# VectorE's waits on itself in the branch kernels of a hybrid decoder trunk: one signal per group of independent operations

## The reference, cut to what matters

```python
u = hn @ w_in[l]
ya = _rwkv7(...) * silu(ag)      # branch A
yb = _hgrn2(...) * silu(bg)      # branch B
yc = _retention(...) * silu(cg)  # branch C
yd = _rglru(...) * silu(dg)      # branch D
merged = sum(merge_gates[:, :, b_i] * (branches[b_i] @ w_branch[l, b_i]) for b_i in range(N_BRANCH))
h = h + gate[:, None, :] * (merged @ w_out[l])
return _rmsnorm(h, final_g)
```

```python
rel = jnp.where(causal, b[:, :, :, None, :] - b[:, :, None, :, :], -jnp.inf)
scores = jnp.sum(q_c[:, :, :, None, :] * k_c[:, :, None, :, :] * jnp.exp(rel), -1)
o = einsum('bhts,bhsv->bhtv', scores, v_c) + einsum('bhtk,bhkv->bhtv', q_c * jnp.exp(b), S)
S = jnp.exp(b_end)[:, :, 0, :, None] * S + einsum('bhsk,bhsv->bhkv', k_c * jnp.exp(b_end - b), v_c)
```

## Time and profile before

| what | value |
|---|---|
| median of three runs | 1161.91 us (1161.1 to 1162.35) |
| time of the profiled execution | 1158.29 us |
| its span, first to last instruction | 1156.1 us |
| mean granted TensorE clock | 0.986 of full speed |
| busy, share of the span | TensorE 93%, weight loads 72%, VectorE 54%, ScalarE 28%, GpSimd 31% |

### The profile page before, as it was taken

The page is one execution under the profiler, slowest core; times in us unless marked ns, Lnnn a source line. Parts: engine busy times, 40 slices in busy tenths (PEclk is TensorE's granted clock), DMA queues, the critical chain, the costliest instruction groups (busy, mean ns, idle before and its releaser), DMA issues.

```text
span 1156.1 us, 23105 instructions
## 1 busy us (share of the span) xinstructions
PE 1072.9 (93%) x9924; PEld 833.6 (72%) x9924; DVE 629.2 (54%) x1033; ACT 327.6 (28%) x527; POOL 361.5 (31%) x347
## 2 busy tenths in 40 slices
PE   1799999989889999999999999999989889999997
PEld 1577786767667777777777787777777767887885
DVE  5773943785463433444443118569999676423544
ACT  4615213311322122122131034144354341001311
POOL 0442543221356222222221233342222138662000
PEclk9999999899999999999999999999999999999999
DMA  9411111110101011011110121111111017412221
GB/s 381 150 37 37 46 55 46 57 35 23 33 25 39 25 34 39 26 32 39 34 35 23 38 64 37 37 56 34 39 34 38 26 31 259 142 37 92 73 91 54
DMA packets 80101, 70.27 MB, mean 61 GB/s; under 512 B 4096, under 2 KB 72960, under 8 KB 78976
## 3 DMA queue, kind: packets, MB, share of 16 engines
q1 hardware_dynamic: 74528, 49.34, 13.7%
q10 hardware_dynamic: 5472, 19.47, 4.6%
HBM read 64.60 MB, written 4.19 MB: 60 GB/s over the span
## 4 chain that ended last, share of the span: by engine, by line
PE 72%; DVE 21%; ACT 3%; DMA 2%; issue 2%; SPq 0%; POOL 0%; DVEq 0%; ACTq 0%
PE bank L553 46%; PE bank L969 8%; PE bank L599 6%; DMA slots<-in_w_mod 1%; DVE slots L1899 1%; DVE slots L1727 1%; DVE slots L1477 1%; DVE slots L1530 1%; DVE slots L1633 1%; PE bank L788 1%; DVE stage L1873 1%; DVE stage L1631 1%; PE bank L784 1%; DMA slots<-in_x 1%; DVE stage L1867 1%
## 5 line engine op out<-in xcount | busy, mean ns | idle before, releaser
L553 PE MATMUL bank<-hn_hi,w_hi 128*128 128x512 f32 x944 | 390.8, 414 | 8.4 <-ACT slots L1038 3.1
L553 PE MATMUL bank<-hn_lo,w_hi 128*128 128x512 f32 x944 | 370.6, 393 | 0.0
L553 PE MATMUL bank<-hn_hi,w_lo 128*128 128x512 f32 x944 | 369.8, 392 | 0.0
L465 POOL CAST w_hi<-w_raw 128x512 fp32r<-128x512 f32 x118 | 82.3, 697 | 650.6 <-PE bank L553 614.8
L553 PEld LDWEIGHTS bank<-hn_hi,w_hi 128*128 128x128 f32 x944 | 178.3, 189 | 54.4 <-issue 7.6
L553 PEld LDWEIGHTS bank<-hn_hi,w_lo 128*128 128x128 f32 x944 | 178.5, 189 | 39.3
L553 PEld LDWEIGHTS bank<-hn_lo,w_hi 128*128 128x128 f32 x944 | 178.9, 189 | 33.8 <-issue 1.7
L467 POOL TENSOR_TENSOR w_lo<-w_raw,w_hi 128x512 fp32r<-128x512 f32 x118 | 161.0, 1364 | 9.4
L1060 ACT ACTIVATE stage<-bank 128x512 f32<-128x512 f32 x64 | 38.3, 598 | 219.3 <-PE bank L553 183.3
L1038 ACT ACTIVATE slots<-bank 128x512 f32<-128x512 f32 x50 | 29.9, 598 | 159.8 <-PE bank L553 159.5
L1631 DVE TENSOR_TENSOR stage<-stage,bank 128x512 f32<-128x512 f32 x48 | 33.0, 687 | 65.4 <-PE bank L599 63.8
(11 more groups left out here) (308 smaller groups left out, 1471.6 us busy)
## 6 DMA issues: line engine op xcount, KB each, us to landing
w_raw<-in_w_in SPq DMA_DIRECT2D x118, 256.0 KB, 2.9
slots<-in_w_mod SPq DMA_DIRECT2D x8, 1024.0 KB, 8.5
slots<-in_x SPq DMA_DIRECT2D x8, 512.0 KB, 7.7
w_branch<-in_w_branch SPq DMA_DIRECT2D x32, 128.0 KB, 2.9
slots<-in_w_mod ACTq DMA_DIRECT2D x8, 512.0 KB, 4.8
slots<-in_w_out ACTq DMA_DIRECT2D x8, 512.0 KB, 5.7
xr<-in_x ACTq DMA_DIRECT2D x8, 512.0 KB, 3.6
out<-xr ACTq DMA_DIRECT2D x8, 512.0 KB, 2.7
```

The lines of the kernel that those rows point to most:

```text
L465: nc.gpsimd.tensor_copy(w_hi[p][:, :, :], w_raw[p][:, :, :]).then_inc(s_w_hi_ready, 1)
L553: last = mm(o, w[p][:, k4, :], h[:, k, n * HALF:(n + 1) * HALF], start=(p == 0 and k4 == 0 and q == 0), stop=(p == 1 and k4 == 3 and q == 2))
```

## The change

VectorE no longer signals and waits after each instruction of the groups named here; within a group it waits only where an instruction reads what an earlier one wrote, and the last instruction of the group signals.

- `prep`: `b_hat` and `k_hat` are written first; `a_r` half 0, the wait for `b_hat`, `b_end`, `a_r` half 1, the wait for `k_hat`, and `k_end` follow.
- The masks `m_all` (L1675) and `Ud` (L1690): one wait, before L1694.
- `u_sb` (L1737) and G (L1749): the increments stay, since TensorE waits for them; VectorE's own waits go.
- `exponents`: one increment and one wait, at L1801. `decayed`: the same, at L1856.
- `h_prod` (L1867): one wait for both halves j. h_s (L1880): VectorE's own waits go.

Counts of TensorE's and ScalarE's waits are the same. No instruction of another engine changes, and no buffer.

```diff
-                nc.vector.tensor_tensor(ar[:, :, :, 0, :], four(4), ep[:, :, :, 0:64], MUL).then_inc(s_vector_step, 1)
-                dve.wait_ge(s_vector_step, after(s_vector_step))
-                nc.vector.tensor_tensor(ar[:, :, :, 1, :], four(8), ep[:, :, :, 1:65], MUL).then_inc(s_vector_step, 1)
-                dve.wait_ge(s_vector_step, after(s_vector_step))
                 nc.vector.tensor_tensor(jc(b_hat), four(14), jc(Em), MUL).then_inc(s_vector_step, 1)
-                dve.wait_ge(s_vector_step, after(s_vector_step))
+                b_done = after(s_vector_step)
                 nc.vector.tensor_tensor(jc(k_hat), four(10), jc(Em), MUL).then_inc(s_vector_step, 1)
-                dve.wait_ge(s_vector_step, after(s_vector_step))
+                k_done = after(s_vector_step)
+                nc.vector.tensor_tensor(ar[:, :, :, 0, :], four(4), ep[:, :, :, 0:64], MUL)
                 e_end = Ep[i % 2][:, :, 64:65].to_broadcast([P, 4, C])
-                nc.vector.tensor_tensor(b_end, b_hat, e_end, MUL).then_inc(s_vector_step, 1)
-                dve.wait_ge(s_vector_step, after(s_vector_step))
+                dve.wait_ge(s_vector_step, b_done)
+                nc.vector.tensor_tensor(b_end, b_hat, e_end, MUL)
+                nc.vector.tensor_tensor(ar[:, :, :, 1, :], four(8), ep[:, :, :, 1:65], MUL)
+                dve.wait_ge(s_vector_step, k_done)
                 nc.vector.tensor_tensor(k_end, k_hat, e_end, MUL).then_inc(s_a_ends_ready, 1)
...
-                                            MUL).then_inc(s_vector_step, 1)
-                    dve.wait_ge(s_vector_step, after(s_vector_step))
+                                            MUL)
...
                                             small_table(tb("up1"), 2), MUL).then_inc(s_vector_step, 1)
-                    dve.wait_ge(s_vector_step, after(s_vector_step))
+                after(s_vector_step)
+                dve.wait_ge(s_vector_step, after(s_vector_step))
...
                                                 ADD).then_inc(s_a_sa_ready, 1)
-                        dve.wait_ge(s_a_sa_ready, after(s_a_sa_ready))
...
                             .then_inc(s_a_g_ready, 1)
-                        dve.wait_ge(s_a_g_ready, after(s_a_g_ready))
...
-                    nc.vector.tensor_tensor(zz[:, :, :, 0:hl], mid, bb[:, :, :, 0:hl], SUB).then_inc(s_vector_step, 1)
-                    dve.wait_ge(s_vector_step, after(s_vector_step))
-                    nc.vector.tensor_tensor(zz[:, :, :, hl:2 * hl], bb[:, :, :, hl:2 * hl], mid, SUB)\
-                        .then_inc(s_vector_step, 1)
-                    dve.wait_ge(s_vector_step, after(s_vector_step))
-                nc.vector.tensor_copy(zd[:, 7, :, :], b).then_inc(s_vector_step, 1)
-                dve.wait_ge(s_vector_step, after(s_vector_step))
+                    nc.vector.tensor_tensor(zz[:, :, :, 0:hl], mid, bb[:, :, :, 0:hl], SUB)
+                    nc.vector.tensor_tensor(zz[:, :, :, hl:2 * hl], bb[:, :, :, hl:2 * hl], mid, SUB)
+                nc.vector.tensor_copy(zd[:, 7, :, :], b)
...
-                nc.vector.tensor_tensor(h_qe[i % 2], zd[:, 7, :, :], q, MUL).then_inc(s_vector_step, 1)
-                dve.wait_ge(s_vector_step, after(s_vector_step))
+                nc.vector.tensor_tensor(h_qe[i % 2], zd[:, 7, :, :], q, MUL)
                 nc.vector.tensor_tensor(zd[:, 8, :, :], zd[:, 8, :, :], k, MUL).then_inc(s_b_z_ready, 1)
...
-                        dve.wait_ge(s_vector_step, after(s_vector_step))
+                    after(s_vector_step)
+                    dve.wait_ge(s_vector_step, after(s_vector_step))
...
                                                    op1=ADD).then_inc(s_b_s_ready, 1)
-                    dve.wait_ge(s_b_s_ready, after(s_b_s_ready))
```

More of the change, by code:

```diff
@@ L1844, in decayed @@
                     qq = q.rearrange("p j (n s) -> p j n s", s=2 * hl)
-                    nc.vector.tensor_tensor(zz[:, :, :, 0:hl], zz[:, :, :, 0:hl], kk[:, :, :, 0:hl], MUL)\
-                        .then_inc(s_vector_step, 1)
-                    dve.wait_ge(s_vector_step, after(s_vector_step))
+                    nc.vector.tensor_tensor(zz[:, :, :, 0:hl], zz[:, :, :, 0:hl], kk[:, :, :, 0:hl], MUL)
                     nc.vector.tensor_tensor(zz[:, :, :, hl:2 * hl], zz[:, :, :, hl:2 * hl],
-                                            qq[:, :, :, hl:2 * hl], MUL).then_inc(s_vector_step, 1)
-                    dve.wait_ge(s_vector_step, after(s_vector_step))
-                nc.vector.tensor_copy(e_last[i % 2], zd[:, 7, :, P - 1:P].rearrange("p j t -> p (j t)"))\
-                    .then_inc(s_vector_step, 1)
-                dve.wait_ge(s_vector_step, after(s_vector_step))
-                nc.vector.tensor_tensor(h_qe[i % 2], zd[:, 7, :, :], q, MUL).then_inc(s_vector_step, 1)
-                dve.wait_ge(s_vector_step, after(s_vector_step))
+                                            qq[:, :, :, hl:2 * hl], MUL)
+                nc.vector.tensor_copy(e_last[i % 2], zd[:, 7, :, P - 1:P].rearrange("p j t -> p (j t)"))
+                nc.vector.tensor_tensor(h_qe[i % 2], zd[:, 7, :, :], q, MUL)
                 nc.vector.tensor_tensor(zd[:, 8, :, :], zd[:, 8, :, :], k, MUL).then_inc(s_b_z_ready, 1)
```

## The result

| | before | changed kernel |
|---|---|---|
| median, first comparison (4 runs each) | 1161.51 us | 1144.49 us (1143.98 to 1147.27) |
| profiled execution, its span | 1158.29, 1156.1 us | 1144.64, 1142.8 us |
| ratio to before, 95% interval | | 0.986, 0.9841 to 0.988 |
| four repeats, 24 runs, medians | 1158.37, 1160.04, 1159.08, 1159.63 us | 1148.04, 1148.27, 1148.27, 1147.56 us |
| ratios of the repeats | | 0.9908, 0.9904, 0.9914, 0.9902 (each within 0.9882 to 0.9931) |

The change is faster. The four repeats gave 10.3, 11.8, 10.8 and 12.1 us off, 11.2 in the mean. So there are two things to explain: the gain, and why one comparison was 6 us beside the repeats.

What follows compares the result with a forecast made beforehand. The prediction took TensorE as the bound, with VectorE late in branch B from pass 1 on. Its terms 9.3 + 1.45 + 0.3 = 11.05 us, off the median of 1161.91, gave 1150.9 us, range 1148.2 to 1156.0.

Steps and rivals of the forecast that it cites:

- The six waits of L929: Branch B: TensorE's waits for ScalarE's L1269, held up by late VectorE, all go: 9.3 us.
- The 1.45 us of clock: Branch B, pass 6: the clock fall behind the longest wait of L929 goes too, 1.45 us.
- The estimate of 0.10 us a wait: Price of one VectorE self-wait, taken below ScalarE's 0.14 us; 35 make 3.5 us a pass of branch B.
- point of saturation: Branch B: the first pass makes up its 1.98 us once each of 35 waits is worth 0.057 us.
- only the gap goes: Rival: one VectorE self-wait is worth 0.03 us, VectorE stays late, 1155.5 us; chance 0.14.
- nothing goes: Rival: VectorE drains between instructions with or without a wait, so the time stays 1161.9 us; chance 0.07.
- slower: Rival: VectorE groups without gaps keep GpSimd out, the weight split is late, TensorE waits: 1164.9 us; chance 0.03.
- 9.7 us of room: Branch B: time from the end of GpSimd's weight split to its first use; only a longer hold costs.
- forecast 0.3: Branch A, pass 0: three fewer self-waits on VectorE's way to L1696, 0.3 us, between 0 and 0.57.
- costed at nothing: Branch A, passes 1 to 7: 14 self-waits a pass go or move, covered by TensorE's fill, worth nothing.
- the low end of the range: 1148.2 us: adds 0.27 us in branch A, another 1.45 us of clock and 1 us of scatter.
- The sum, 11.05 us: Whole kernel: 9.3 for waits of L929, 1.45 for clock, 0.3 for branch A's pass 0; chance 0.74.

Runs made afterwards that it cites:

- masks_only: The kernel before with only the self-waits of the masks m_all and Ud in branch A removed: 1157.6 us, ratio 0.9986.
- before_again: The kernel before, run and profiled once more with nothing changed: 1158.6 us, ratio 1.0.
- b_rep: Repeat of the kernel before with only branch B's edits (exponents, decayed, h_prod, h_s): 1147.2 us, ratio 0.9902.
- exp_only: The kernel before with only the self-waits of branch B's exponents removed, 15 a pass: 1150.8 us, ratio 0.9927.
- dec_only: The kernel before with only the self-waits of branch B's decayed operands removed, 16 a pass: 1148.7 us, ratio 0.992.
- a_only: The kernel before with only branch A's edits (prep, masks, Ud, u_sb, G): 1156.5 us, ratio 0.998.
- b_only: The kernel before with only branch B's edits (exponents, decayed, h_prod, h_s): 1145.8 us, ratio 0.9883.

## Why the prediction was right or wrong

**Right: where the time goes.** The six waits of L929 are gone; pass 0 to pass 6 shortened by 9.14 us, forecast 9.3. The last pass, with the longest wait and the clock fall behind it, shortened by (144.10 - 122.97) - (133.60 - 113.83) = 1.36 us, forecast 1.45. Together 10.5 us, forecast 10.75. The passes take 18.97 us in the mean, forecast 18.9, though not all are near it (18.42 to 19.83), and the clock of the stretch is 1.00. No wait of L929 for another engine took the place. The 1.45 us of clock came out by luck, in part: the forecast read them from one execution. With the same waits of L929 or nearly, masks_only had no fall in B, and before_again had two; b_rep, without these waits, had one.

**Right: that the exact price hardly matters, but its size was low.** The estimate of 0.10 us a wait measured 0.12. exp_only (15 waits, 1.85 us by that price) and dec_only (16, 1.97 us) each bring nearly all that 35 waits bring, and keep 2.7 and 1.7 us of waits. The forecast put the point of saturation at 0.057 us for each of 35 waits, 1.98 us a pass in the first pass; both stand right at it. Nothing of the rivals "only the gap goes" and "nothing goes" is left: the starts moved by 0.12 us, not by 0.03 or 0. The rival "slower" was wrong in its size and not in its mechanism. GpSimd's records in B are longer (44 of 50.43 us in all, where 43 of 35.28 us stood), and the traces show where: a cast of L465 that starts within the group L1838 and L1839 takes 2.17 us, where the casts of the kernel before took 0.61 to 0.76.

```profile
796.19 2.17 POOL L465 CAST w_hi<-w_raw 128x512 fp32r<-128x512 f32 x1 [7.78 <-PE bank L553]
```

In all five profiles of the changed kernel five or six of B's casts take 2.1 to 2.2 us. So a group without waits does keep GpSimd back, by 1.6 us here, against the 9.7 us of room that the prediction read; no L553 or L599 waits for it there.

"VectorE: DVE Perf Modes" of the Trainium skill, section "The DRAIN you can't avoid", would by its eight copies have made the gain zero; for tensor_tensor of 128 columns this trace differs, and the measurement decides. The same section also says that a next operation that is not held starts earlier, which the prediction left out; the 375 overlapping records agree with that. The estimate from the Trainium skill's "Vector Engine (DVE) Microarchitecture Reference", section "Measured stream behaviour on trn2", 208 ns from start to start, agrees with the 203 measured.

**Right, but seen in the traces alone: branch A.** In pass 0 from the first L1674 to L1695 VectorE now takes 1.91 us, and it took 2.30: 0.39 us sooner, forecast 0.3. These are the rows of the changed kernel:

```profile
307.66 1.29 DVE L1674 TENSOR_TENSOR stage<-bank,tab 128x512 f32<-128x512 f32 x2 [4.05 <-PE bank L753]
...
309.57 0.31 DVE L1695 STREAM_TRANSPOSE stage<-stage 128x128 f32<-128x128 f32 x1
...
309.94 0.45 PE L784 MATMUL bank<-stage 32*32 32x32 f32 x32 [0.45 <-DVE stage L1695]
```

TensorE's wait there fell from 0.84 to 0.45 us. The table of the head shows the same 0.4 us where the clock is alike: from L688 to L784, 62.2 us became 61.8 at a clock of 0.91, and 64.9 became 64.5 at 0.75 to 0.79. masks_only and a_only take 61.8 us there, b_only 62.2, so it comes from branch A's hunks, and masks_only has them at the masks alone. The 14 waits a pass in passes 1 to 7, costed at nothing, cost nothing that shows: from the first L784 to the first L929 it is 469.7 and 469.6 us in the two profiles of before, 469.0 to 471.4 in the five of the changed kernel. The stretch of the earlier trace rows from 345 to 645 us, in the changed kernel and 3.8 us sooner, has the same 298.97 us of TensorE, and 108.19 us of VectorE instead of 115.81:

```profile
341.20:641.20 300.00, 298.97 (x4421) 223.40 (x4420) 108.19 (x304) 66.81 (x125) 81.28 (x91) 1.00 0.11 32
```

**Wrong: the step from the sum to the median, and the low end of the range.** The sum, 11.05 us, is what the repeats measured (11.2 in the mean; all four intervals of the ratio hold 1150.9 / 1161.91 = 0.9905). The step that failed is the one that says that the profiled execution "is 3.6 us below the median, which I carry over", with "1 us of scatter between executions". That took the three runs of before, 1.25 us apart, for the spread of the kernel. The later runs spread from 1151.69 to 1165.81 us for the kernel before, and from 1144.99 to 1151.67 for the changed one. The head alone took 309.0 to 317.6 us over the 13 profiles whose kernels leave TensorE's work there as it was. And the range was hung on 1161.91 us, 2.6 above the mean of before's medians in the repeats (1159.3), so even there, with the gain as forecast, two of the four medians (1148.04 and 1147.56 us) lie just below its low end of 1148.2. Of the 5.8 us by which the first comparison exceeds the mean of the repeats, 3.5 lie in a changed kernel faster than its repeats (1144.49 against their mean median of 1148.0) and 2.2 in a kernel before that was slower than in the repeats (1161.51 against 1159.3).

The last part of the tail also moved by clock. In the first profile of the changed kernel the wait for L1633 came with a longer fall (of TensorE's timeline; a 512-column matmul takes 0.39 us at the full level):

```profile
939.08 0.47 PE L599 MATMUL bank<-y_hi,w_branch_hi 128*128 128x512 f32 x1 [3.68 <-DVE slots L1633]
...
941.47 0.77 PE L599 MATMUL bank<-y_hi,w_branch_hi 128*128 128x512 f32 x1 [0.62 <-DVE slots L1633]
...
946.73 0.63 PE L553 MATMUL bank<-hn_hi,w_hi 128*128 128x512 f32 x1
```

It gave 1.8 us back (230.3 us behind B instead of 228.5); over all kernels that part takes 226.9 to 230.3 us. The prediction's sentence that what lies behind the loop "move[s] with them as a whole" is right for the work and wrong for the clock.

**What stays open.** That falls of the clock set the length of the head is shown: the waits are the same, the time differs in the three stretches where the clock does, and covering a wait brings the head forward. Three of the four runs of the changed kernel in the first comparison lay below all 24 runs of the repeats; their mean granted clock is on record as 0.988 and 0.989, and no run of the repeats has more than 0.986. So these were executions with little low clock. Why so many of the four were is open: it may be the chip or chance, and no kernel here tells these apart.

## What to carry to other kernels

Ask of a wait on an engine's own result whether it is on a path where the next engine waits, and how much that path must shorten before another engine is the bound: here 1.9 of 4.3 us a pass brought most of the gain. Where TensorE stands still, count the fall of the clock behind the wait as well, read from more than one execution, and put work that is due anyway into the wait. Look, too, at what runs beside a group that loses its waits: GpSimd's cast, 0.61 to 0.76 us before, takes 2.17 us beside it now. A forecast in per mille needs the spread over chips and executions; three close runs don't give it, and a stretch of the trace ahead of the change, compared between two executions, does.

## What was not expected of the hardware

- Behind the same waits (9.7 us or a little more ahead of L628, then 2.5 ahead of L619) the clock fell not at all, or for long: its mean from 40 to 65 us was 1.00, 0.86, 0.77, 0.86 and 0.71 in the five profiles of the changed kernel. Low clock ahead of 50 us cost nothing (177.0 us to L658 at 0.77 as at 1.00), behind 50 us it cost 2 us (178.9 at 0.86). Their heads end up to 7.1 us apart.
- 73 transposes whose result nobody reads, and 12 matmuls put forward, together brought about as much as the change itself: 21.4 us faster than before with all of it, 11.2 us by the change alone.
- Two VectorE instructions without a wait between them overlap in the records: 0.28 us long, 0.203 us apart, for 128 columns. While such a group runs, a GpSimd cast took 2.17 us instead of 0.61.
